# The final weighted sums: the first 512 columns on TensorE, the other 512 on VectorE

## The reference, cut to what matters

```python
# _moe: comb holds, for each token, the weights of its two experts
for e in range(N_EXPERTS):
    a = jax.nn.silu(hf @ w_gate[e]) * (hf @ w_up[e])
    y = y + comb[:, e:e + 1] * (a @ w_down[e])
# the layer
x = x + g2[:, None, :] * _moe(h, w_router, router_bias, w_gate_e[l], w_up_e[l], w_down_e[l])
# _rmsnorm of the result, with g = final_norm_g
y = xf * lax.rsqrt(jnp.mean(xf * xf, axis=-1, keepdims=True) + EPS) * g
```

## Time and profile before

| | |
|---|---|
| median of 3 runs | 876.65 us (876.29 to 877.86) |
| the profiled execution, its own time | 877.76 us |
| span of its records | 875.9 us |
| PE busy | 818.2 us (93%) |
| DVE busy | 474.8 us (54%) |
| ACT busy | 202.0 us (23%) |
| last scatter landed, first load of the tail issued | 851.98 us |
| last DVE instruction starts | 871.59 us |

### The profile page before, as it was taken

How to read it: one execution, slowest core, us unless ns; L and a number is a source line. 1 busy time by engine, 2 the same in 40 slices (tenths; PEclk the granted TensorE clock), 3 DMA queues, 4 the chain that set the end, 5 groups by cost and what they waited for, 6 DMA issues and landing times.

```text
span 875.9 us, 14246 instructions
## 1 busy us (share of the span) xinstructions
PE 818.2 (93%) x5766; PEld 599.1 (68%) x5766; DVE 474.8 (54%) x637; ACT 202.0 (23%) x261; POOL 142.8 (16%) x200
## 2 busy tenths in 40 slices
PE   2899999999999999999999999889999999999960
PEld 0578889889799878787888899655555555555530
DVE  3649996987698965878777655701111111111117
ACT  3441211122422134622222342200000000000012
POOL 0000321321323200410000000022222222222220
PEclk9999998999999999999999999999999999999995
DMA  9923231212121121258775758998999999998316
GB/s 316 369 75 97 96 97 49 98 49 96 49 97 50 54 93 49 98 192 281 247 240 192 263 194 337 400 381 333 337 394 396 399 391 400 395 395 308 134 35 278
DMA packets 102207, 191.59 MB, mean 219 GB/s; under 512 B 4151, under 2 KB 41287, under 8 KB 102161
## 3 DMA queue, kind: packets, MB, share of 16 engines
q1 hardware_dynamic: 89042, 160.79, 50.6%
q10 hardware_dynamic: 9168, 19.40, 6.6%
q0 software_dynamic: 3952, 10.76, 3.4%
HBM read 182.54 MB, written 10.49 MB: 220 GB/s over the span
## 4 chain that ended last, share of the span: by engine, by line
PE 84%; DVE 6%; DMA 3%; SPq 3%; issue 2%; ACT 1%; POOL 0%; ACTq 0%; DVEq 0%; POOLq 0%
PE proj L874 19%; PE proj L572 15%; PE proj L574 14%; PE proj L573 14%; PE ha L910 10%; PE pp L678 2%; SPq L476 2%; DMA ada_w<-in_w_ada 2%; PE pp L864 2%; PE ha L896 1%; SPq L479 1%; PE pp L656 1%; PE ha L708 1%; PE pp L733 1%; PE ha L745 1%
## 5 line engine op out<-in xcount | busy, mean ns | idle before, releaser
L874 PE MATMUL proj<-ew,heT 128*64 128x256 f32 x1536 | 175.0, 381 | 0.7 <-ACT heT L1140 0.7
L874 PEld LDWEIGHTS proj<-ew,heT 128*64 128x64 f32 x1536 | 108.7, 137 | 65.4 <-issue 16.4
L572 PE MATMUL proj<-h_hi,w_hi 128*128 128x512 f32 x368 | 146.2, 397 | 3.8 <-DVE h_lo L1242 3.2
L574 PE MATMUL proj<-h_hi,w_lo 128*128 128x512 f32 x368 | 143.4, 390 | 0.0
L573 PE MATMUL proj<-h_lo,w_hi 128*128 128x512 f32 x368 | 143.3, 389 | 0.0
L1364 DVE SCALAR_TENSOR_TENSOR acc<-u_t,cols_t,acc 128x512 f32<-128x512 f32 x120 | 91.1, 808 | 0.6
L1201 DVE TENSOR_TENSOR w_lo<-w_raw,w_hi 128x2048 fp32r<-128x2048 f32 x35 | 80.2, 2291 | 15.8 <-ACT w_hi L957 15.8
L910 PE MATMUL ha<-ew,aT 128*64 128x512 f32 x384 | 87.7, 598 | 0.9 <-DVE aT L1719 0.9
L957 ACT ACTIVATE w_hi<-w_raw 128x2048 fp32r<-128x2048 f32 x36 | 68.7, 1909 | 69.6 <-PE proj L574 44.9
L572 PEld LDWEIGHTS proj<-h_hi,w_hi 128*128 128x128 f32 x368 | 69.1, 188 | 22.5 <-issue 8.4
L574 PEld LDWEIGHTS proj<-h_hi,w_lo 128*128 128x128 f32 x368 | 69.1, 188 | 14.6
(11 more groups left out here) (254 smaller groups left out, 1237.3 us busy)
## 6 DMA issues: line engine op xcount, KB each, us to landing
ew<-in_w_gate SPq DMA_DIRECT2D x32, 1024.0 KB, 15.2
ew<-in_w_up SPq DMA_DIRECT2D x32, 1024.0 KB, 15.2
ew<-in_w_down SPq DMA_DIRECT2D x32, 1024.0 KB, 14.5
w_raw<-in_w_in SPq DMA_DIRECT2D x28, 1024.0 KB, 5.1
ada_p<-in_w_ada ACTq DMA_DIRECT2D x16, 1024.0 KB, 5.2
ada_w<-in_w_ada SPq DMA_DIRECT2D x8, 1024.0 KB, 13.7
w_raw<-in_w_o_hgrn SPq DMA_DIRECT2D x4, 1024.0 KB, 5.5
w_raw<-in_w_out SPq DMA_DIRECT2D x4, 1024.0 KB, 10.0
```

The source lines that it names most:

```text
L572: pe.matmul(outap, a_hi, b_hi, start=first, stop=False)
L574: return pe.matmul(outap, a_lo, b_hi, start=False, stop=last)
L874: mm = pe.matmul(out_ps[JS * i:JS * i + JS, 0:FG], heT[:, c_, JS * j_:JS * j_ + JS], w[:, k, FG * i:FG * i + FG], start=(kb == 0), stop=(k ...
```

## The change

TensorE takes the first 512 columns of each sum, as three matmuls that add up in one PSUM bank (`half_sum[tt]`): the identity with x2, a diagonal matrix of w0 with y0, a diagonal matrix of w1 with y1. VectorE keeps columns 512 to 1023. The eight diagonal matrices (`w_diag`) are made by one more DVE instruction, behind the routing. ACT squares the two halves apart: the SBUF half first, whose mean plus epsilon an added Identity activation makes, and then the PSUM half; the root takes the first as its bias. DVE scales a tile in two instructions, one reading PSUM and one reading SBUF. PE issues the four x2 matmuls behind the last job, then 42 matmuls of `busy`, then the eight diagonal ones. DVE's order becomes: sum 0, sum 1, sum 2, scale 0, sum 3, scale 1, scale 2, scale 3. Two semaphores of the index table are made one (`s_oh1` goes into `s_oj`), which frees a semaphore and moves no instruction.

```diff
+        w_diag = at("w_diag", "K", [P, 2 * TT, P], F32, 4096)
...
+        half_sum = [proj[:, 0, :], proj[:, 1, :], pp[:, 0:512], pp[:, 512:1024]]
@@ sync
-                sp.wait_ge(s_fo, tt + 1)
+                sp.wait_ge(s_fo, 2 * tt + 2)
@@ tensor
             def table():
-                pe.wait_ge(s_oh1, 1)
-                pe.wait_ge(s_oj, 1)
+                pe.wait_ge(s_oj, 2)
@@ tensor, behind the last down
+            pe.wait_ge(s_sg, last * LANES + LANES)
+            pe.wait_ge(s_he, last * LANES + (LANES + 1))
+            for tt in range(TT):
+                pe.matmul(half_sum[tt], ident, x2_t[:, tt, 0:512], start=True, stop=False)
+            busy(ha[:, 3, :], 42)
+            pe.wait_ge(s_wd, 1)
+            for tt in range(TT):
+                pe.wait_ge(s_fl[tt], 16)
+                pe.matmul(half_sum[tt], w_diag[:, tt, :], fin[tt][:, 0, 0:512], start=False, stop=False)
+                pe.matmul(half_sum[tt], w_diag[:, TT + tt, :], fin[tt][:, 1, 0:512], start=False, stop=True).then_inc(s_fp, 1)
@@ scalar, for tt in range(TT)
                 act.wait_ge(s_f2, tt + 1)
                 if tt:
-                    act.wait_ge(s_fa, 2 * tt - 1)
-                act.activation(fsq[:, :], fin[tt][:, 1, :], ACT.Square, accum_out=nst[:, tt:tt + 1]).then_inc(s_fa, 1)
-                act.wait_ge(s_fa, 2 * tt + 1)
-                act.activation(nst[:, 4 + tt:5 + tt], nst[:, tt:tt + 1], ACT.Sqrt, scale=1.0 / D,
-                               bias=eps_c[:, 0:1]).then_inc(s_fa, 1)
+                    act.wait_ge(s_fa, 4 * tt - 1)
+                act.activation(fsq[:, 512:1024], fin[tt][:, 1, 512:1024], ACT.Square, accum_out=nsq[:, tt, 0:1]).then_inc(s_fa, 1)
+                act.wait_ge(s_fa, 4 * tt + 1)
+                act.activation(nsq[:, tt, 1:2], nsq[:, tt, 0:1], ACT.Identity, scale=1.0 / D, bias=eps_c[:, 0:1]).then_inc(s_fa, 1)
+                act.wait_ge(s_fp, tt + 1)
+                act.activation(fsq[:, 0:512], half_sum[tt], ACT.Square, accum_out=nsq[:, tt, 2:3]).then_inc(s_fa, 1)
+                act.wait_ge(s_fa, 4 * tt + 3)
+                act.activation(nst[:, 4 + tt:5 + tt], nsq[:, tt, 2:3], ACT.Sqrt, scale=1.0 / D,
+                               bias=nsq[:, tt, 1:2]).then_inc(s_fa, 1)
@@ vector, behind the index table
+            dve.tensor_tensor(w_diag[:, :, :], ident.rearrange("p (o n) -> p o n", o=1).broadcast_to([P, 2 * TT, P]),
+                              wsel[:, :, :].rearrange("p a (b o) -> p (a b) o", o=1).broadcast_to([P, 2 * TT, P]),
+                              ALU.mult).then_inc(s_wd, 1)
@@ vector, the tail
+            def final_sum(tt):
+                half = slice(512, 1024)
+                dve.wait_ge(s_fl[tt], 16)
+                dve.scalar_tensor_tensor(fin[tt][:, 0, half], fin[tt][:, 0, half], wsel[:, 0, tt:tt + 1], x2_t[:, tt, half],
+                                         ALU.mult, ALU.add).then_inc(s_f1, 1)
+                dve.wait_ge(s_f1, tt + 1)
+                dve.scalar_tensor_tensor(fin[tt][:, 1, half], fin[tt][:, 1, half], wsel[:, 1, tt:tt + 1], fin[tt][:, 0, half],
+                                         ALU.mult, ALU.add).then_inc(s_f2, 1)
+            def final_scale(tt):
+                dve.wait_ge(s_fa, 4 * tt + 4)
+                dve.reciprocal(nst[:, 4 + tt:5 + tt], nst[:, 4 + tt:5 + tt]).then_inc(s_fr, 1)
+                dve.wait_ge(s_fr, tt + 1)
+                dve.scalar_tensor_tensor(fin[tt][:, 0, 0:512], half_sum[tt], nst[:, 4 + tt:5 + tt], gfin[:, 0:512],
+                                         ALU.mult, ALU.mult).then_inc(s_fo, 1)
+                dve.wait_ge(s_f2, tt + 1)
+                dve.scalar_tensor_tensor(fin[tt][:, 0, 512:1024], fin[tt][:, 1, 512:1024], nst[:, 4 + tt:5 + tt],
+                                         gfin[:, 512:1024], ALU.mult, ALU.mult).then_inc(s_fo, 1)
+            final_sum(0)
+            final_sum(1)
+            final_sum(2)
+            final_scale(0)
+            final_sum(3)
+            for tt in range(1, TT):
+                final_scale(tt)
```

More of the change, by code:

```diff
@@ L327, in trunk_kernel @@
         s_pt = sem("part_numbers_set")
-        s_oh1 = sem("places_one_hot")
-        s_oj = sem("jobs_one_hot")
+        s_oj = sem("places_and_jobs_one_hot")
         s_ix = sem("index_table_done")
@@ L357, in trunk_kernel @@
         s_fr = sem("final_root_inverted")
+        s_wd = sem("pair_weight_diagonals")
+        s_fp = sem("final_first_half_summed")
         s_fo = sem("final_done")
@@ L1645, in _ @@
             dve.tensor_tensor(slot1[:, :, :], io[:, 0:JS].rearrange("p (o s) -> p o s", o=1).broadcast_to([P, 2 * TT, JS]),
-                              col(r(18, 0, 8)).broadcast_to([P, 2 * TT, JS]), ALU.is_equal).then_inc(s_oh1, 1)
+                              col(r(18, 0, 8)).broadcast_to([P, 2 * TT, JS]), ALU.is_equal).then_inc(s_oj, 1)
             settle()
@@ L1743, in _ @@
             dve.wait_ge(s_gl, 16)
-            for tt in range(TT + 1):
-                if tt < TT:
-                    dve.wait_ge(s_fl[tt], 16)
-                    dve.scalar_tensor_tensor(fin[tt][:, 0, :], fin[tt][:, 0, :], wsel[:, 0, tt:tt + 1], x2_t[:, tt, :],
-                                             ALU.mult, ALU.add).then_inc(s_f1, 1)
-                    dve.wait_ge(s_f1, tt + 1)
-                    dve.scalar_tensor_tensor(fin[tt][:, 1, :], fin[tt][:, 1, :], wsel[:, 1, tt:tt + 1], fin[tt][:, 0, :],
-                                             ALU.mult, ALU.add).then_inc(s_f2, 1)
-                if tt:
-                    q = tt - 1
-                    dve.wait_ge(s_fa, 2 * q + 2)
-                    dve.reciprocal(nst[:, 4 + q:5 + q], nst[:, 4 + q:5 + q]).then_inc(s_fr, 1)
-                    dve.wait_ge(s_fr, q + 1)
-                    dve.wait_ge(s_f2, q + 1)
-                    dve.scalar_tensor_tensor(fin[q][:, 0, :], fin[q][:, 1, :], nst[:, 4 + q:5 + q], gfin[:, :],
-                                             ALU.mult, ALU.mult).then_inc(s_fo, 1)
+            def final_sum(tt):
[6 more added lines that the diff above has]
+                                         ALU.mult, ALU.add).then_inc(s_f2, 1)
```

## The result

The changed kernel takes 880.53 us, the median of 20 runs (879.16 to 884.44), against 876.61 us for the kernel before in 20 runs of the same session. One of the 20 runs of before took 1412.26 us and is outside the ratio. The ratio is 1.0029, with a 95% interval of 1.0015 to 1.0043. (The two medians alone give 1.0045; 15 of the other 19 runs of before lie between 875.92 and 878.12 us and four between 880.21 and 882.86, so its median says little of the upper ones.) The changed kernel is slower, by 0.15% to 0.43%, and its time lies outside the range that I gave. The profiled execution took 881.18 us (877.76 before), its span 879.3 us (875.9 before).

What follows compares the result with a forecast made beforehand. The tail was taken as bound by DVE, with the loads the other limit. Halved sums less dearer scales and 0.4 us of PE lateness end DVE 1.8 us sooner: 874.9 us from the median 876.65, range 873.8 to 876.8.

Steps and rivals of the forecast that it cites:

- The diagonals: Added DVE instruction before the expert loop's first product: 1.22 us, hidden by DVE's 3.82 us wait for PE, taken as 0.
- my three rivals: Waits between engines eat the gain (chance 0.20), TensorE at half rate in the tail (0.08), a larger gain (0.10).
- The sign that I had named: Expert loop's start: a later L1733 product of the first lane would show the zero cost of the diagonals wrong.
- The loads land 4.8 us ... 11.0 us after their issue: Tail loads: the first lands 4.8 us and the last 11.0 us after issue, as in the kernel before.
- PE's lateness: Tail, tile 0: diagonal matmuls wait for busy, so DVE's first reciprocal starts 0.4 us later than the loads alone allow.
- VectorE's scales: Tail, scale cut in two: 0.19 + 0.60 + 0.66 = 1.45 us a tile, where it was 1.39; PSUM read 0.68 us long.
- the half-rate rival: Tail: PE at the lower clock, diagonal matmuls 2.0 us each, DVE ends 6.7 us later, 883.4 us; chance 0.08.
- The sums: Tail, VectorE's sum of one tile on half the columns: 0.75 + 0.04 + 0.66 = 1.45 us, where it was 2.52.
- the links rival: Tail: four more waits a tile make DVE wait for each root; gain 0.1 to 1.0 us, about 876.0; chance 0.20.
- my 1.77: Tail's forecast gain: DVE's last instruction ends at 871.1 instead of 872.87, given as 1.8 us less.
- The bound of 0.2%: Whole kernel: about 0.2%, 1.75 us, is what a measurement can tell from no change; the 1.8 us gain stands there.

Runs made afterwards that it cites:

- e2: Kernel before plus the DVE instruction that makes the diagonals, read by nobody, with the two semaphores merged; median 881.89 us, ratio 1.0062 to before.
- e9: Kernel before with merged semaphores plus an unread DVE copy of 1024 columns from PSUM where the change makes the diagonals; median 877.46 us, ratio 1.0001 to before.
- e3: Kernel before plus an unread POOL memset ahead of the first spacer, nothing added on DVE; median 880.21 us, ratio 1.0017 to before.
- e6: Changed kernel plus 15 unread busy matmuls in PE's wait for the first gather; median 878.35 us, ratio 0.9999 to before.
- e1: Changed kernel with the diagonals made behind DVE's first lane of job 0 instead of ahead of it; median 877.33 us, ratio 0.9991 to before.
- e4: As e1, with 11 matmuls of 512 columns in place of the 42 busy ones of 128; median 878.16 us, ratio 1.0005 to before.
- e10: Kernel before plus four unread float32 matmuls of 128 x 512 and 42 busy ones behind the last down; median 880.44 us, ratio 1.0027 to before.
- e5: As e1, with 28 busy matmuls ahead of the x2 matmuls instead of 42 behind them; median 876.70 us, ratio 0.9980 to before.

## Why the prediction was wrong

**The diagonals: the step that failed.** "What hides it is that wait; without the wait it would cost its 1.22 us once. I take 0." The wait did hide it from DVE's own work, with 2.48 us left. But a cover on the instruction's own engine says nothing of the engine beside it. POOL's one-column multiplication met it and lasted 1.18 us (e2), not 0.19 (e9). The gather behind it was issued 0.74 us later and its data came 1.75 us later. The clock fell in the longer wait. Price in the profile: 4.08 us in after and 3.96 in e2, while e2's ratio of 1.0062 is 5.4 us. None of my three rivals held it. The sign that I had named, a later product in the first lane, didn't show either: it started at 573.08 us (573.24 before), and the loss came behind it.

That the later issue costs more than itself shows in the table: with the spacer long, or POOL delayed in e3, 5.6 to 6.3 us pass from the gather's issue to T1; otherwise 4.5 to 5.6. From T0 to T1 the mean is 13.14 us in these four kernels and 11.27 in the eight others. SP issues its next weight loads at a time of its own. In before the gather's issue on POOL ended at 571.14, ahead of SP's at 571.44; in after it ended at 571.88, behind SP's at 571.36. SP's rows, before and after:

```profile
571.44 0.97 SPq L457 DMA_DIRECT2D ew<-in_w_gate  x2
```

```profile
571.36 0.98 SPq L460 DMA_DIRECT2D ew<-in_w_gate  x2
```

The order is the same in all twelve profiles: behind SP's in after, e2, e3 and e6, ahead of it in the eight others. That the gather's rows then stand behind the weights' is argued, not shown: no run moved the weight loads.

**That a wait of this length lets the clock fall, always: not shown.** In the profiles it fell behind waits of 1.57 (e9), 2.00 (e1) and 2.33 us (e4), and all those above 3.5 (after, e2, e3), but not behind 1.60 (before), 1.84 (e10) and 2.63 (e5). In the middle it seems to be open from run to run: e1 and e4 have runs at 875 and at 880. What the change did is to make it frequent. None of the 20 runs of after is below 879.16 us or above a mean clock of 0.992, while e1 has seven below 878, five of them at 0.994. Why it falls in one execution and not in the next stays open.

**"The loads land 4.8 us ... 11.0 us after their issue": carried over, and wrong by 1.2 us.** This term of the sum came from before's rows. The longer PE program brought an instruction packet among them, shown by e10 (21.99 us with PE's work alone) and from the other side by e6 (19.46 us when the packet comes early). Of the 1.2 us, 0.86 reached the end: the first reciprocal starts 12.63 us behind the first load's issue (868.69 less 856.06), where I had 11.77. PE's lateness, for which I had 0.4 us, then lay behind the loads and cost nothing. The Trainium skill's "Runtime: NRT & Kernel Launch" (section "Instruction fetch mechanics") says that instructions arrive in blocks of 16 KiB by a DMA queue, and that this is mostly hidden. The size agrees with the packet's 0.02 MB. By e10 and e4 it isn't hidden from the transfers that it meets.

**VectorE's scales: a term mis-sized.** I took the PSUM read at 0.68 us long and 0.60 from start to start. L1777 lasts 0.75 us, and the next instruction starts 0.66 or 0.67 us after it (868.88 to 869.55). That is 0.06 us a tile, 0.25 us in all. The instruction whose row I took multiplies by a constant; L1777 multiplies by a column of SBUF in its place, as the SBUF rows of 0.75 us do. By "VectorE: DVE Perf Modes" (section "The TRN2 errata") of the Trainium skill I had put 0.5 us against the change. About half of that came, and not as a difference of PSUM from SBUF: L1777 on PSUM takes 0.75 us and L1780 on SBUF 0.74. Both terms together are the difference: 19.12 us forecast for the tail, plus 0.86, plus 0.25, is 20.23.

**What was right.** The x2 matmuls start 4.04 us ahead of the first load's issue (forecast 4.1) and busy takes 9.54 us (9.4). The first diagonal matmul comes 8.87 us behind that issue (8.7), its records are 0.43 us apart, and the clock is 1.00: the half-rate rival fell. The sums take 0.75 + 0.04 + 0.66 us, as forecast. ACT takes 1.86 us for one tile and 1.84 for the next (866.86, 868.72 and 870.56 are the starts of its Squares on PSUM; forecast 1.86), so the links rival fell too: in after DVE never waited for a root, and in e6, with the loads in time, 0.29 us once. Without the packet the change is worth 1.43 us in the tail (e6), 0.34 less than my 1.77, and 0.25 of that is the PSUM read. Two small figures of my sum stood in no row that I showed: the 0.62 us of a lone Square (0.63 in before's trace, at 12.89) and the 0.1 us until ACT sees PE's result (0.04 after the modelled end of the last record). Neither changes it.

**The bound of 0.2%.** A gain of 1.4 to 1.8 us at best stands against 1.7 us for each stretch of low clock, of which a run of this kernel may have two to six, an estimate from the mean clocks of 0.982 to 0.973. A forecast for such a kernel needs a term for how the change shifts these stretches, and mine had none.

## What to carry to other kernels

An instruction that is free on its own engine can still hold another one: look at what the neighbour that shares a port with it (here GpSimd beside VectorE) has to do in the same microsecond, above all if that is a tiny instruction ahead of a gather. Instructions added to an engine are fetched by DMA, so look which transfer the added block will meet, and shift it to where nothing waits for a landing. Where a wait lets the clock fall, try dummy matmuls in it: the three kernels that had them kept the clock in their profiles, though only e6 starts from a kernel whose profile shows the fall. A list of mean clocks beside the run times shows how much of a spread they explain.

## What the runs showed of the hardware that I had not expected

- A GpSimd multiplication of 128 x 1 lasts 0.19 us alone and 1.18 us beside a VectorE tensor_tensor of 1024 columns with two SBUF inputs (after, e2, e6); beside a VectorE copy from PSUM of the same 1.23 us it lasts 0.19 us (e9).
- One instruction packet of 16 KB among loads spread over 16 engines makes the load that it meets, and those behind it, 1.1 to 1.2 us late (after, e10, e4), and a scatter of 2.24 us 1.15 us longer (e5).
- PE's granted clock is at 0.50 for 3.4 or 6.8 us behind some waits (from 1.57 us up) and in or behind 32 matmul records of one column each, in which PE counts as busy. The places recur, and how many such stretches there are changes from run to run; each 3.4 us cost 1.7 us.
- A scalar_tensor_tensor of 512 float32 columns takes 0.75 us with one operand in PSUM and a column and a row block in SBUF, 0.74 to 0.75 us with all in SBUF, and 0.68 us with one in PSUM and a constant in place of the column.
